# Layer norms of a transformer's second block: a shifted running sum on GpSimd, the last and first tile less the shift, one root, and another order of tiles

## The chip, the cores and the metric

The kernel runs on one core of a Trainium2 chip. The metric is the device time of one execution in microseconds, as the median of several runs. PE is the matrix engine (TensorE), DVE the vector engine (VectorE), ACT the scalar engine (ScalarE), POOL GpSimd, and SP the engine that issues the loads of weights.

## The reference, cut to what matters

Two blocks follow one another on 256 tokens of width 1024. The first (two mixers with RMS norms, two MLPs) is not touched. The second puts 16 meta tokens in front, which makes 272, and normalizes with means:

```python
def layer_norm(x, g, b):
    mu = jnp.mean(xf, -1, keepdims=True)
    var = jnp.mean(jnp.square(xf - mu), -1, keepdims=True)
    return (xf - mu) * lax.rsqrt(var + LN_EPS) * g + b

h = layer_norm(concat([meta, x]), emb_ln_g, emb_ln_b)         # mean_e
for i in range(2):
    u = h @ w_in[i]
    ...                                                       # attention and conv (with a norm of its own)
    h = layer_norm(ALPHA * h + mix, ln1_g[i], ln1_b[i])       # n10, n11
    f = swiglu(h, ...) if i == 0 else moe_swiglu(h, router, ...)
    h = layer_norm(ALPHA * h + f, ln2_g[i], ln2_b[i])         # n2, and the last norm
```

## The kernel before, in words

Activations lie with the 1024 features on partitions, as 8 tiles of 128 features by T = 272 tokens (RES holds the residual, XC centred tiles, SQ squares and normed tiles, RS the running sum). A sum over features is therefore a matmul with a matrix of ones, which leaves the sum over a tile's 128 features in every partition of a PSUM bank.

Weights stream through as 311 units of 1 MB, each 16 tiles of 128x128. ACT makes the high half `wh` of a unit (L1221) and DVE the low half `wl` (L1721, "the split"); three buffers hold them. A product is three matmuls (wh with the high half of x, wh with its low half, wl with the high half), 272 columns each. `gemm_lead` (L472 to L485) starts a gemm behind a norm: it takes tile 0 of the norm as soon as its high half is there (L472, L473), then its low half (L476), and then tile by tile the three products for four output tiles (L483 to L485). Further units go through L523 to L525.

There is no scheduler: each engine has a program of its own (`tensor_program`, `scalar_program`, `vector_program`, `gpsimd_program`, `sync_program`), in which the instructions stand in the order in which they run, with semaphore waits (`w.wait_ge(*m.of(...))`) between the engines. On DVE and ACT a split of the next unit is entered between the steps of a norm by the helper `sp` (`take`, `enter`, `hold`).

Four norms run through `shifted_norm`: mean_e behind the first block's last gemm, n10 and n11 behind the output gemms of the two layers (L2191 adds the bank into RES), n2 behind the dense feed-forward (L2216). They go in these steps:

- When tile 0 is in RES, a matmul sums it over the features, and ACT makes SH from it, the shift: the mean of tile 0 per token.
- For each tile DVE takes the shift off (L1940), ACT squares (L1402), and POOL adds: tiles into RS (L2548) and squares into SQ[0] (L2553).
- At the end PE's `last_sums` sums RS (L773) and the last tile (L778) into the mean's bank, and the squares (L780, L782) into the variance's. `keep_warm` (L431) issues products that nobody reads, to fill PE's waiting time: 1 and then 11.
- DVE makes d = mean - SH and d squared (L1955, L1957), v = variance + eps - d squared (L1960), and the first two centred tiles (L1950). ACT takes Ln and Exp (L1407, L1409) for a first value of the root, and DVE one Newton step (L1964 to L1968).
- DVE then makes each tile's normed value (L1973), centres a later tile (L1950), and makes the low half of the one before (L1985); ACT makes the high half (L1416). In n11 ACT writes RES instead (L1447), and the router follows on PE (L925 to L943).

`last_norm` at the end of the program (L1432 to L1440, L2001 to L2031) and the norms of the two conv layers (L1523, L1525) also take the root by Ln and Exp.

Of the kernel before, what the change touches and what calls it, by code (L numbers as in the profile page):

```python
# [11 lines left out]
ALU = mybir.AluOpType  # L12
# [3 lines left out]
P = 128  # L16
# [146 lines left out]
LOG_EXP = "natural_log_exp_and_others"  # L163
HUGE = 3.0e38
# [25 lines left out]
def model_kernel(nc, w_d, x_d, meta_d, small_d, const_d, look_d, out_d):  # L190
# [3 lines left out]
    with ctx:  # L194
# [206 lines left out]
        def tensor_program(w, pe):  # L401
# [354 lines left out]
            def shift_sum(stage, name):  # L756
                def pump(nt):
                    if nt == 2:
                        b, old = bank((name, "shift"), ("shift", name))
# [7 lines left out]
            def last_sums(stage, name):  # L767
                b, old = bank((name, "mean"), ("centred", (name, KD - 1)))
                if name == "n11":
                    held.add(b)  # L770
                vacant(old)
                w.wait_ge(*m.of("res_added", (name, KD - 2)))
# [432 lines left out]
        def scalar_program(w, act):  # L1205
# [187 lines left out]
            def shifted(name, nt):  # L1393

                if nt == 3:
                    w.wait_ge(*m.of("group", (name, "shift")))
                    act.activation(SH, bank((name, "shift"))[:, 0:T], ACT.Copy, scale=1.0 / P).then_inc(*m.inc("shift", name))
                if nt == KD - 1:
                    act.preload_act_table_set(LOG_EXP)
# [24 lines left out]
            def last_norm(tag, sem, keys):  # L1424
                act.preload_act_table_set(LOG_EXP)
# [9 lines left out]
                act.activation(SQ[:, 6, M:T], SQ[:, 5, M:T], ACT.Ln).then_inc(*m.inc("last_guess", "log"))  # L1435
                w.wait_ge(*m.of("last_guess", "log"))
                act.activation(BC[:, M:T], SQ[:, 6, M:T], ACT.Exp, scale=-0.5).then_inc(*m.inc("last_guess", "root"))
# [11 lines left out]
            def mix_layer(l):  # L1449
# [67 lines left out]
                act.preload_act_table_set(LOG_EXP)  # L1517
# [1223 lines left out]
```

## Time and profile before

| | us |
|---|---|
| median of 3 runs (1646.05 to 1647.68) | 1647.63 |
| the profiled execution's own time | 1647.6 |
| its span, from first to last instruction | 1645.8 |
| PE busy | 1614.5 (98%) |
| DVE busy | 1241.6 (75%) |
| ACT busy | 970.0 (59%) |
| POOL busy | 304.2 (18%) |
| mean granted clock of PE | 0.999 |

The time of an execution is 1.8 us longer than its span. Busy shares are means over the whole program; a norm is some ten microseconds, so it is read in the timeline of its own stretch. PE's busy time counts the products of `keep_warm`. In the timeline a line shows the start, the duration (for several instructions together their stretch), engine, line and operation, and in brackets the idle time ahead of it and what ended it; "x22" counts records, of which one fp32 matmul has two.

### The profile page before, as it was taken

Reading aid. Unit: us, or ns where it says so; the run is one execution under the profiler, and the core shown is the slowest. Engines: PE = TensorE matmul, PEld = TensorE weight load, DVE = VectorE, ACT = ScalarE, POOL = GpSimd, SP = SyncE. Lnnn points to the kernel's source line nnn. Section 1 sums busy time; section 2 is a strip of 40 time slices with the busy share of each in tenths; the row PEclk is TensorE's granted clock in tenths of the full one; section 3 lists DMA queues with packets and bytes.
Section 4 is the critical chain, followed back from the end, with each engine's and each line's share of the span. In section 5 each row is a group of like instructions: output and inputs, shape, how many; then the busy total and the mean of one; then the engine's idle time right before and its main releaser. Section 6 shows DMA issues by size and latency. Waiting matters only on the chain.

```text
span 1645.8 us, 27513 instructions
## 1 busy us (share of the span) xinstructions
PE 1614.5 (98%) x11020; PEld 1472.9 (89%) x11020; DVE 1241.6 (75%) x1766; ACT 970.0 (59%) x1377; POOL 304.2 (18%) x301
## 2 busy tenths in 40 slices
PE   7999999999999999999999999999999999999997
PEld 7988888898888889989999999999988888888886
DVE  6655776665667656998975545899988899998897
ACT  6556674346657633555554433555558677776775
POOL 1230652123226402052210002131110000000000
PEclk9999999999999999999999999999999999999999
DMA  7732455554245555433435444533439899988983
GB/s 282 255 126 80 179 197 188 197 206 162 103 159 195 185 179 211 164 132 126 154 132 201 171 175 169 180 143 136 173 118 342 332 341 343 340 334 332 351 340 125
DMA packets 50020, 339.73 MB, mean 206 GB/s; under 512 B 5403, under 2 KB 7611, under 8 KB 10208
## 3 DMA queue, kind: packets, MB, share of 16 engines
q1 hardware_dynamic: 47344, 328.79, 54.4%
q0 software_dynamic: 2544, 9.12, 1.7%
q8 instruction: 90, 1.47, 0.3%
q14 instruction: 42, 0.34, 0.1%
HBM read 336.76 MB, written 1.13 MB: 205 GB/s over the span
## 4 chain that ended last, share of the span: by engine, by line
PE 87%; DVE 4%; issue 4%; ACT 2%; POOL 2%; DMA 1%; SPq 0%; POOLq 0%; DVEq 0%; ACTq 0%
PE bank L549 12%; PE bank L523 8%; PE bank L525 8%; PE bank L524 8%; PE bank L547 7%; PE bank L979 5%; PE bank L980 5%; PE bank L981 5%; PE bank L1012 2%; PE bank L1011 2%; PE bank L1010 2%; PE bank L676 2%; PE bank L678 2%; PE bank L677 2%; PE bank L431 1%
## 5 line engine op out<-in xcount | busy, mean ns | idle before, releaser
L1721 DVE TENSOR_TENSOR wl<-stg,wh 128x2048 fp32r<-128x2048 f32 x310 | 712.7, 2302 | 208.1 <-ACT wh L1221 206.0
L1221 ACT ACTIVATE wh<-stg 128x2048 fp32r<-128x2048 f32 x310 | 592.8, 1913 | 178.9 <-PE bank L981 82.7
L523 PE MATMUL bank<-xx,wh 128*128 128x272 f32 (+1 forms) x778 | 225.3, 290 | 0.0
L525 PE MATMUL bank<-xx,wl 128*128 128x272 f32 (+1 forms) x778 | 223.1, 287 | 0.0
L524 PE MATMUL bank<-xx,wh 128*128 128x272 f32 (+1 forms) x778 | 223.0, 287 | 0.0
L549 PE MATMUL bank<-xx,wh 128*128 128x512 f32 x448 | 159.7, 396 | 0.0
L549 PE MATMUL bank<-H,wh 128*128 128x512 f32 x434 | 151.3, 390 | 0.0
L979 PE MATMUL bank<-wh,GH 128*128 128x512 f32 (+3 forms) x400 | 147.5, 369 | 0.0
L523 PEld LDWEIGHTS bank<-xx,wh 128*128 128x128 f32 x778 | 146.4, 188 | 1.1 <-issue 0.7
L524 PEld LDWEIGHTS bank<-xx,wh 128*128 128x128 f32 x778 | 147.4, 189 | 0.0
L525 PEld LDWEIGHTS bank<-xx,wl 128*128 128x128 f32 x778 | 146.4, 188 | 0.0
L980 PE MATMUL bank<-wh,GL 128*128 128x512 f32 (+3 forms) x400 | 146.3, 366 | 0.0
L981 PE MATMUL bank<-wl,GH 128*128 128x512 f32 (+3 forms) x400 | 146.2, 366 | 0.0
L676 PE MATMUL bank<-wh,xx 128*128 128x256 f32 x480 | 139.8, 291 | 1.0 <-DVE zm L1795 1.0
L678 PE MATMUL bank<-wl,xx 128*128 128x256 f32 x480 | 135.0, 281 | 0.0
L677 PE MATMUL bank<-wh,xx 128*128 128x256 f32 x480 | 134.7, 281 | 0.0
L547 PE MATMUL bank<-xx,wl 128*128 128x256 f32 x512 | 132.4, 279 | 0.0
L547 PE MATMUL bank<-H,wl 128*128 128x256 f32 x448 | 123.9, 282 | 0.0
L2523 POOL TENSOR_TENSOR fu<-ft 128x256 f32<-128x256 f32 x64 | 85.0, 1331 | 132.7 <-ACT ft L1369 132.7
L2081 DVE SCALAR_TENSOR_TENSOR CA<-HC,small,CA 128x272 f32<-128x272 f32 x240 | 107.6, 502 | 0.7
L547 PEld LDWEIGHTS bank<-xx,wl 128*128 128x128 f32 x512 | 96.5, 188 | 5.9 <-issue 0.3
L549 PEld LDWEIGHTS bank<-xx,wh 128*128 128x128 f32 x448 | 84.1, 188 | 17.2
(382 smaller groups left out, 3537.2 us busy)
## 6 DMA issues: line engine op xcount, KB each, us to landing
stg<-in_w SPq DMA_DIRECT2D x310, 1024.0 KB, 4.9
BT<-bias_scratch POOLq DMA_DIRECT2D x3, 1024.0 KB, 11.3
BT<-bias_scratch POOLq DMA_DIRECT2D x1, 2048.0 KB, 12.2
BB<-bias_scratch POOLq DMA_DIRECT2D x2, 1024.0 KB, 6.3
res<-in_x SPq DMA_DIRECT2D x1, 1024.0 KB, 7.2
stg<-in_w SPq DMA_DIRECT2D x2, 512.0 KB, 8.0
BB<-bias_scratch POOLq DMA_DIRECT2D x2, 512.0 KB, 7.1
out<-res SPq DMA_DIRECT2D x4, 256.0 KB, 3.3
```

Of the source, the lines that this page charges most:

```text
L523: pe.matmul(out, wh, xh(kt), start=kt == 0, stop=False)
L524: pe.matmul(out, wh, xl(kt), start=False, stop=False)
L525: ins = pe.matmul(out, wl, xh(kt), start=False, stop=kt == KT - 1)
L547: ins = pe.matmul(PS[b][:, 0:S], wl, high(kt), start=False, stop=False)
L549: ins = pe.matmul(out, wh, both(kt), start=False, stop=kt == KT - 1)
L676: pe.matmul(out, xh_t(kt, tt), wh, start=kt == 0, stop=False)
L678: ins = pe.matmul(out, xh_t(kt, tt), wl, start=False, stop=kt == KD - 1)
L979: pe.matmul(out, lh(kt, i), wh, start=kt == 0, stop=False)
L980: pe.matmul(out, ll(kt, i), wh, start=False, stop=False)
L981: ins = pe.matmul(out, lh(kt, i), wl, start=False, stop=kt == KD - 1)
L1221: act.activation(WH[u % NW][:, :], stg[u % NS][:, :], ACT.Copy).then_inc(*m.inc("w_high", u))
L1721: vec.tensor_tensor(WL[u % NW][:, :], stg[u % NS][:, :], WH[u % NW][:, :].bitcast(F32), ALU.subtract).then_inc(*m.inc("w_low_v", u))
```

## The change

In the four norms through `shifted_norm`:

- ACT makes two more copies of the shift: XC[3] = -7 SH, and XC[5] = 8 SH. POOL adds XC[3] into RS after tile 5, so that RS, with the tiles 0 to 6, holds their sum less seven shifts.
- After tile 6 DVE makes XC[6] = (ALPHA times) RES[7] - SH ahead of the last product (`less_shift`) and XC[2] = RES[0] - SH. When the last bank is there, `last_tile` adds it into XC[6]; the residual itself comes behind it. ACT squares XC[6] directly.
- PE sums RS and XC[6] into a bank "less", which is the sum over all features less the shift 1024 times. ACT squares its mean (into BC), and DVE needs only that for v; L1955 and L1957 are gone. A second bank, "mean", gets RS, XC[5] and XC[6]. `keep_warm` comes once, with 4.
- ACT takes one `Abs_reciprocal_sqrt` in place of Ln and Exp, here and in the conv norms and the last norm; the table set loaded in these places is another one.
- Tile 0 is centred from "less" (`first_tile`), ahead of the root; all others behind the root, each right before its normed value, in the order n0, c1, n1, low0, c2, n2, low1, and so on.

```diff
@@ last_sums (PE)
-                b, old = bank((name, "mean"), ("centred", (name, KD - 1)))
...
-                w.wait_ge(*m.of("res_added", (name, KD - 2)))
+                b, old = bank((name, "less"), ("centred", (name, 0)))
+                w.wait_ge(*m.of("res_added", (name, "shifted")))
                 pe.matmul(PS[b][:, 0:T], ones, RS, start=True, stop=False)
...
-                keep_warm(1)
-                w.wait_ge(*m.of("res", (stage, KD - 1)))
-                pe.matmul(PS[b][:, 0:T], ones, RES[:, KD - 1, 0:T], start=False, stop=True).then_inc(*m.inc("group", (name, "mean")))
                 w.wait_ge(*m.of("sq_added", (name, KD - 2)))
                 pe.matmul(PS[v][:, 0:T], ones, SQ[:, 0, 0:T], start=True, stop=False)
+                w.wait_ge(*m.of("last_tile", name))
+                pe.matmul(PS[b][:, 0:T], ones, XC[:, KD - 2, :], start=False, stop=True).then_inc(*m.inc("group", (name, "less")))
                 w.wait_ge(*m.of("shifted_sq", (name, KD - 1)))
                 pe.matmul(PS[v][:, 0:T], ones, SQ[:, KD - 1, 0:T], start=False, stop=True).then_inc(*m.inc("group", (name, "var")))
-                keep_warm(11)
+                f, old = bank((name, "mean"), ("centred", (name, KD - 1)))
...
+                w.wait_ge(*m.of("shift_8", name))
+                pe.matmul(PS[f][:, 0:T], ones, RS, start=True, stop=False)
+                pe.matmul(PS[f][:, 0:T], ones, XC[:, KD - 3, :], start=False, stop=False)
+                pe.matmul(PS[f][:, 0:T], ones, XC[:, KD - 2, :], start=False, stop=True).then_inc(*m.inc("group", (name, "mean")))
+                keep_warm(4)
@@ shifted, guess (ACT)
+                    act.activation(XC[:, 3, :], bank((name, "shift"))[:, 0:T], ACT.Copy, scale=(1.0 - KD) / P).then_inc(*m.inc("shift_7", name))
                 if nt == KD - 1:
-                    act.preload_act_table_set(LOG_EXP)
+                    act.preload_act_table_set(ROOT)
...
+                    act.activation(XC[:, KD - 3, :], SH, ACT.Copy, scale=float(KD)).then_inc(*m.inc("shift_8", name))
+                    w.wait_ge(*m.of("last_tile", name))
+                    act.activation(SQ[:, KD - 1, :], XC[:, KD - 2, :], ACT.Square, scale=D ** -0.5).then_inc(*m.inc("shifted_sq", (name, KD - 1)))
+                    return
...
             def guess(name):
+                w.wait_ge(*m.of("group", (name, "less")))
+                act.activation(BC[:, :], bank((name, "less"))[:, 0:T], ACT.Square, scale=1.0 / D).then_inc(*m.inc("mean_sq", name))
                 w.wait_ge(*m.of("var_out", name))
-                act.activation(SQ[:, 3, :], SQ[:, 2, :], ACT.Ln).then_inc(*m.step("table"))
-                w.wait_ge(*m.last("table"))
-                act.activation(BC[:, :], SQ[:, 3, :], ACT.Exp, scale=-0.5).then_inc(*m.inc("guess", name))
+                act.activation(BC[:, :], SQ[:, 2, :], ACT.Abs_reciprocal_sqrt).then_inc(*m.inc("guess", name))
@@ less_shift, last_tile, shifted_norm (DVE)
+                    ins = vec.scalar_tensor_tensor(XC[:, KD - 2, :], RES[:, KD - 1, :], scale, SH, ALU.mult, ALU.subtract)
+                ins.then_inc(*m.inc("less_shift", name))
+                vec.tensor_tensor(XC[:, 2, :], RES[:, 0, :], SH, ALU.subtract).then_inc(*m.inc("first_less", name))
...
+                vec.tensor_tensor(XC[:, KD - 2, lo:T], XC[:, KD - 2, lo:T], part, ALU.add).then_inc(*m.inc("last_tile", name))
...
-                vec.scalar_tensor_tensor(v, var, LN_EPS, d, ALU.add, ALU.subtract).then_inc(*m.inc("var_out", name))
-                centre(0)
-                centre(1)
+                vec.scalar_tensor_tensor(v, var, LN_EPS, BC[:, :], ALU.add, ALU.subtract).then_inc(*m.inc("var_out", name))
+                first_tile()
...
                     if kt == 0:
-                        centre(2)
-                    if 2 <= kt < KD - 1:
-                        centre(kt + 1)
+                        w.wait_ge(*m.of("group", (name, "mean")))
+                        centre(1)
                     if kt > 0:
                         low(kt - 1)
+                    if 0 < kt < KD - 1:
+                        centre(kt + 1)
@@ running (POOL)
                     pool.tensor_tensor(RS, RES[:, 0, :] if nt == 1 else RS, RES[:, nt, :], ALU.add).then_inc(*m.inc("res_added", (name, nt)))
+                    if nt == KD - 3:
+                        w.wait_ge(*m.last("res_added"))
+                        w.wait_ge(*m.of("shift_7", name))
+                        pool.tensor_tensor(RS, RS, XC[:, 3, :], ALU.add).then_inc(*m.inc("res_added", (name, "less")))
```

In the order of instructions the place is n10, between the output gemm's tile 6 and the first step behind the root. On DVE (xc is XC, dg the memory of SH, bank a PSUM bank), before:

```order
L2191 SCALAR_TENSOR_TENSOR res<-res,bank 128x272
L1940 TENSOR_TENSOR sq<-res,dg 128x272
L1721 TENSOR_TENSOR wl<-stg,wh 128x2048
L2191 SCALAR_TENSOR_TENSOR res<-res,bank 128x272
L1940 TENSOR_TENSOR sq<-res,dg 128x272
L1955 SCALAR_TENSOR_TENSOR sq<-bank,dg 128x272
L1957 TENSOR_TENSOR sq<-sq 128x272
L1960 SCALAR_TENSOR_TENSOR sq<-bank,sq 128x272
L1950 SCALAR_TENSOR_TENSOR xc<-bank,res 128x272 x2
L1964 TENSOR_TENSOR sq<-bc 128x272
```

and of the changed kernel, from the same tile 6 on:

```order
L2225 SCALAR_TENSOR_TENSOR res<-res,bank 128x272
L1958 TENSOR_TENSOR sq<-res,dg 128x272
L1967 SCALAR_TENSOR_TENSOR xc<-res,dg 128x272
L1969 TENSOR_TENSOR xc<-res,dg 128x272
L1733 TENSOR_TENSOR wl<-stg,wh 128x2048
L1974 TENSOR_TENSOR xc<-xc,bank 128x272
L2225 SCALAR_TENSOR_TENSOR res<-res,bank 128x272
L1992 SCALAR_TENSOR_TENSOR sq<-bank,bc 128x272
L1986 SCALAR_TENSOR_TENSOR xc<-bank,xc 128x272
L1995 TENSOR_TENSOR sq<-bc 128x272
```

Two steps that read the residual and the shift stand ahead of the split now, and behind the last tile only v and one centred tile stand ahead of the Newton step. On POOL in the same norm, before, from the addition of tile 4 on:

```order
L2548 TENSOR_TENSOR xc<-xc,res 128x272
L2553 TENSOR_TENSOR sq<-sq 128x272 x2
L2548 TENSOR_TENSOR xc<-xc,res 128x272
L2553 TENSOR_TENSOR sq<-sq 128x272
L2548 TENSOR_TENSOR xc<-xc,res 128x272
```

and of the changed kernel:

```order
L2590 TENSOR_TENSOR xc<-xc,res 128x272
L2601 TENSOR_TENSOR sq<-sq 128x272 x2
L2590 TENSOR_TENSOR xc<-xc,res 128x272
L2594 TENSOR_TENSOR xc<-xc 128x272
L2601 TENSOR_TENSOR sq<-sq 128x272
L2590 TENSOR_TENSOR xc<-xc,res 128x272
```

The addition L2594 stands between the sum of tile 5 and its square. On ACT one table load is added, in the router ahead of its Exp.

## Rows read from the trace of the kernel before

**Rows 1.** The page: parts 1 and 5 (columns: count; busy us, mean ns; idle before, releaser).

```profile
PE 1614.5 (98%) x11020; PEld 1472.9 (89%) x11020; DVE 1241.6 (75%) x1766; ACT 970.0 (59%) x1377; POOL 304.2 (18%) x301
...
L1721 DVE TENSOR_TENSOR wl<-stg,wh 128x2048 fp32r<-128x2048 f32 x310 | 712.7, 2302 | 208.1 <-ACT wh L1221 206.0
L1221 ACT ACTIVATE wh<-stg 128x2048 fp32r<-128x2048 f32 x310 | 592.8, 1913 | 178.9 <-PE bank L981 82.7
```

**Rows 2.** Timeline of mean_e: start us, us, engine, line, operation [idle before].

```profile
654.46 0.42 DVE L1921 TENSOR_TENSOR xc<-bank,bc 128x256 f32<-128x256 f32 x1 [1.30 <-PE bank L525]
...
656.90 4.91 PE L431 MATMUL bank<-consts 128*128 128x256 f32 x22
657.18 0.44 DVE L1960 SCALAR_TENSOR_TENSOR sq<-bank,sq 128x272 f32<-128x272 f32 x1
...
657.65 0.43 ACT L1407 ACTIVATE sq<-sq 128x272 f32<-128x272 f32 x1 [1.37 <-DVE sq L1960]
658.11 0.43 ACT L1409 ACTIVATE bc<-sq 128x272 f32<-128x272 f32 x1
...
660.00 0.50 DVE L1973 SCALAR_TENSOR_TENSOR sq<-xc,small,bc 128x272 f32<-128x272 f32 x1
...
663.15 0.29 PE L483 MATMUL bank<-xx,wh 128*128 128x272 f32 x1
```

**Rows 3.** Timeline of n2.

```profile
1034.92 0.62 PE L773 MATMUL bank<-xc,consts 128*128 128x272 f32 x2
...
1040.28 0.50 DVE L1973 SCALAR_TENSOR_TENSOR sq<-xc,small,bc 128x272 f32<-128x272 f32 x1
...
1043.44 0.29 PE L483 MATMUL bank<-xx,wh 128*128 128x272 f32 x1
```

**Rows 4.** Timeline of n10, on VectorE, GpSimd and TensorE.

```profile
824.21 0.51 DVE L1940 TENSOR_TENSOR sq<-res,dg 128x272 f32<-128x272 f32 x1
...
824.64 2.85 DVE L1721 TENSOR_TENSOR wl<-stg,wh 128x2048 fp32r<-128x2048 f32 x1
...
825.31 2.80 POOL L2548 TENSOR_TENSOR xc<-xc,res 128x272 f32<-128x272 f32 x1
...
828.26 0.70 PE L773 MATMUL bank<-xc,consts 128*128 128x272 f32 x2 [1.53 <-POOL xc L2548]
...
830.87 0.44 DVE L1960 SCALAR_TENSOR_TENSOR sq<-bank,sq 128x272 f32<-128x272 f32 x1
...
836.85 0.29 PE L483 MATMUL bank<-xx,wh 128*128 128x272 f32 x1
```

**Rows 5.** Timeline of n11 and the router's first products.

```profile
1198.26 0.76 POOL L2553 TENSOR_TENSOR sq<-sq 128x272 f32<-128x272 f32 x1
...
1201.05 0.44 DVE L1960 SCALAR_TENSOR_TENSOR sq<-bank,sq 128x272 f32<-128x272 f32 x1
...
1210.04 0.52 ACT L1447 ACTIVATE res<-sq,small 128x272 f32<-128x272 f32 x1 [0.37 <-DVE sq L1973]
...
1211.42 0.51 PE L925 MATMUL bank<-small,res 128*128 128x8 f32 x4
```

**Rows 6.** Timeline of ScalarE: a table load, its next instruction, and the router's Exp.

```profile
671.84 1.28 ACT L1487 ACT_TABLE_LOAD   x1
673.14 0.40 ACT L1487 ACTIVATE HC<-bank 128x272 f32<-128x272 f32 x1
...
1214.66 0.21 ACT L1573 ACTIVATE C<-C 128x2 f32<-128x2 f32 x1 [1.45 <-DVE C L2267]
```

**Rows 7.** Timeline of the last norm: VectorE's first step behind Exp.

```profile
1635.85 0.43 DVE L2015 TENSOR_TENSOR sq<-bc 128x256 f32<-128x256 f32 x1 [0.33 <-ACT bc L1437]
```

**Rows 8.** Granted clock (the number before the DMA share) by windows, and line L439.

```profile
826.00:828.00 2.00, 0.72 (x6) 0.50 (x4) 1.97 (x3) 0.48 (x1) 2.00 (x1) 1.00 0.56 238
1642.00:1643.00 1.00, 0.00 (x0) 0.00 (x0) 0.00 (x0) 0.00 (x0) 0.00 (x0) 0.68 0.72 242
...
L439 PE MATMUL bank<-res x10: 634/634/796, 8.4 to 12.4; 128*128 128x256 f32 x10
```

More of the change, by code:

```diff
@@ L758, in pump @@
                     if nt == 2:
-                        b, old = bank((name, "shift"), ("shift", name))
+                        b, old = bank((name, "shift"), ("shift_7", name))
                         vacant(old)
@@ L1434, in last_norm @@
                 w.wait_ge(*m.of("last_v"))
-                act.activation(SQ[:, 6, M:T], SQ[:, 5, M:T], ACT.Ln).then_inc(*m.inc("last_guess", "log"))
-                w.wait_ge(*m.of("last_guess", "log"))
-                act.activation(BC[:, M:T], SQ[:, 6, M:T], ACT.Exp, scale=-0.5).then_inc(*m.inc("last_guess", "root"))
+                act.activation(BC[:, M:T], SQ[:, 5, M:T], ACT.Abs_reciprocal_sqrt).then_inc(*m.inc("last_guess", "root"))
                 for kt in range(6):
@@ L1522, in silu @@
                     w.wait_ge(*m.of("var_out", name))
-                    act.activation(SQ[:, 5, :], SQ[:, 4, :], ACT.Ln).then_inc(*m.step("table"))
-                    w.wait_ge(*m.last("table"))
-                    act.activation(BC[:, :], SQ[:, 5, :], ACT.Exp, scale=-0.5).then_inc(*m.inc("guess", name))
+                    act.activation(BC[:, :], SQ[:, 4, :], ACT.Abs_reciprocal_sqrt).then_inc(*m.inc("guess", name))
                     sp.one_ahead()
@@ L1929, in evac_y @@
                         shifted("mean_e", nt)
+                        if nt == KD - 2:
+                            less_shift("mean_e", None)
                 walk(KD, 32, evac_y)
@@ L1937, in shifted @@
                     w.wait_ge(*m.of("shift", name))
+                if nt == KD - 1:
+                    return
                 for kt in SHIFTED.get(nt, ()):
@@ L1942, in shifted, with less_shift @@
                     sp.hold()
+            def less_shift(name, scale):
+                if scale is None:
+                    ins = vec.tensor_tensor(XC[:, KD - 2, :], RES[:, KD - 1, :], SH, ALU.subtract)
+                else:
+                    ins = vec.scalar_tensor_tensor(XC[:, KD - 2, :], RES[:, KD - 1, :], scale, SH, ALU.mult, ALU.subtract)
+                ins.then_inc(*m.inc("less_shift", name))
+                vec.tensor_tensor(XC[:, 2, :], RES[:, 0, :], SH, ALU.subtract).then_inc(*m.inc("first_less", name))
@@ L1944, in shifted_norm, with last_tile @@
+            def last_tile(name, part, lo):
+                w.wait_ge(*m.of("less_shift", name))
+                vec.tensor_tensor(XC[:, KD - 2, lo:T], XC[:, KD - 2, lo:T], part, ALU.add).then_inc(*m.inc("last_tile", name))
             def shifted_norm(name, gname, l, low):
-                d, v, t = SQ[:, 1, :], SQ[:, 2, :], SQ[:, 3, :]
-                mean, var = bank((name, "mean"))[:, 0:T], bank((name, "var"))[:, 0:T]
+                v, t = SQ[:, 2, :], SQ[:, 3, :]
+                less, mean, var = (bank((name, part))[:, 0:T] for part in ("less", "mean", "var"))
@@ L1949, in centre, with first_tile @@
                 def centre(kt):
                     vec.scalar_tensor_tensor(XC[:, kt, :], mean, -1.0 / D, RES[:, kt, 0:T], ALU.mult, ALU.add).then_inc(*m.inc("centred", (name, kt)))
+                def first_tile():
+                    w.wait_ge(*m.of("first_less", name))
+                    vec.scalar_tensor_tensor(XC[:, 2, :], less, -1.0 / D, XC[:, 2, :], ALU.mult, ALU.add).then_inc(*m.inc("centred", (name, 0)))
                 w.wait_ge(*m.last("res"))
-                w.wait_ge(*m.of("group", (name, "mean")))
@@ L1954, in shifted_norm @@
                 w.wait_ge(*m.of("sq_added", (name, KD - 2)))
-                vec.scalar_tensor_tensor(d, mean, 1.0 / D, SH, ALU.mult, ALU.subtract).then_inc(*m.step("v_step"))
-                w.wait_ge(*m.last("v_step"))
-                vec.tensor_tensor(d, d, d, ALU.mult).then_inc(*m.step("v_step"))
-                w.wait_ge(*m.last("v_step"))
+                w.wait_ge(*m.of("mean_sq", name))
                 w.wait_ge(*m.of("group", (name, "var")))
-                vec.scalar_tensor_tensor(v, var, LN_EPS, d, ALU.add, ALU.subtract).then_inc(*m.inc("var_out", name))
@@ L2193, in evac_o @@
                     shifted(f"n1{l}", nt)
+                    if nt == KD - 2:
+                        w.wait_ge(*m.of("y_out", (before, KD - 1)))
+                        less_shift(f"n1{l}", ALPHA)
                 walk_late(KD, KD, evac_o)
@@ L2215, in evac_d @@
                     w.wait_ge(*m.of("y_out", ("n10", nt)))
+                    if nt == KD - 1:
+                        last_tile("n2", bank(("dn", nt))[:, 0:T], 0)
                     vec.scalar_tensor_tensor(RES[:, nt, :], RES[:, nt, :], ALPHA, bank(("dn", nt))[:, 0:T], ALU.mult,
@@ L2218, in evac_d @@
                     shifted("n2", nt)
+                    if nt == KD - 2:
+                        w.wait_ge(*m.of("y_out", ("n10", KD - 1)))
+                        less_shift("n2", ALPHA)
                 walk(KD, 22, evac_d)
```

22 lines of the change are left out of this document (17 added, 5 removed).

## The prediction

> **What bounds the kernel now.** I read the page first, then the stretch around each of the four norms in the timeline, then the chain of waits there. TensorE is busy for 98% of the span, and ScalarE's largest wait, before the high halves of the weights, is for a buffer that TensorE still reads (82.7 us of 178.9): matmuls, not DMA, set the pace [rows 1]. So a norm costs what lies between the last product in front of it and the first steady product behind it, and a microsecond saved there carries through to the end. Busy time hides this, because L431 fills the gaps with products that nobody reads.
>
> In mean_e, VectorE was idle for 1.30 us when the last tile's bank came (654.46), v (L1960) starts at 657.18, Ln and Exp follow 0.46 apart, the first normed tile (L1973) starts at 660.00, and the second tile's first full product (L483) at 663.15 [rows 2]. The 22 records of L431 end at 661.81, so the lead could not begin much earlier; yet the second tile, which needs a low half from VectorE, is what starts the steady run. From n0 to it pass 3.15 us here, and 3.16 us in n2 (1040.28 to 1043.44) [rows 2, 3].
>
> n10 is different. VectorE's shift of tile 6 (0.51) is followed at once by a weight split of 2.85 us, against a mean of 2.30 [rows 1, 4]. GpSimd's addition for RS next to it takes 2.80, against 0.76 alone [rows 4, 5]. So the two engines exclude each other while both work from SBUF. TensorE idles 1.53 us for that RS and starts the sums at 828.26. In this norm GpSimd is on the path.
>
> **The change, part by part.** A step of 128x272 takes 0.44 to 0.51 on VectorE and 0.43 on ScalarE, one behind the other every 0.46; GpSimd's addition holds the shared way for about 0.67 of its 0.76 (both [rows 2, 4, 5]; 0.67 is my estimate). A pair of fp32 matmuls takes about 0.46: 22 records of 256 columns take 4.91 [rows 2], a little more at 272.
>
> *One root for Ln and Exp.* The step from L1407 to L1409 is 0.46 [rows 2]. The root's own price is not in the trace. Its nearest rows are Ln, at 0.43 [rows 2], and an activation with a small operand, at 0.52 [rows 5]; below 0.43 it can hardly lie, since the tile is the same. I take 0.43: 0.46 less per norm, at worst 0.37.
>
> *The path to v in mean_e and n2.* Before: scale, residual, L1940, Square, and L1955, L1957, L1960. Now the last tile comes less the shift by one VectorE step (0.46 ahead of the residual), ScalarE squares it, TensorE makes the "less" pair and the last square's pair, ScalarE squares the mean, and v follows. In mean_e: scale 654.46, last tile to 655.36, less pair to about 655.9, the mean's square to 656.45 beside the other pair (which ends near 656.4), v near 656.7 against 657.18: 0.5 less. In n2 the four pairs run in a row from 1034.92 [rows 3], to about 1036.8, and v comes about 0.4 earlier. The two new steps behind tile 6 (less_shift, first_less: 0.9 together) fit into VectorE's idle time there, 1.30 [rows 2]; without that cover they would cost up to 0.9.
>
> *The order of tiles.* Each centre now stands right before its norm, so every norm waits for its centre, and the low half of tile 1 comes ahead of tile 3's centre. I count n0, c1, n1, low0, c2, n2, low1 at the starts of [rows 2] and the same steps' spacing: n0 to low1 2.33, plus its 0.49 and 0.13 for the semaphore, so 2.95 to the second tile, against 3.15. So mean_e gains 0.5 + 0.46 + 0.2 = **1.15**, and n2 0.4 + 0.46 + 0.2, rounded down to **1.0**. The extra products behind the sums are 4 instead of 12, with two pairs more in the mean's group; they end by about 660.0, ahead of the lead at about 660.2, so they hold nothing.
>
> *n10.* Two VectorE steps with two SBUF inputs now stand ahead of the split, and one GpSimd addition ahead of the squares of tile 5. If the engines take turns (as the rows of the split and of RS show), the queue from 824.35 is: shift 6 0.42, new addition 0.67, less_shift 0.49, square 5 0.67, first_less 0.42, RS 0.67, which ends at 827.5 (0.6 earlier than now [rows 4]); then the split to 829.8; then the square of tile 6 to 830.45. The last tile comes only behind the split, at 829.75. The pairs of SQ0, less and the last square start near 830.6, and v at about 832.2, against 830.87 [rows 4]: 1.3 later. Root 0.46 less, so n0 at 834.55. The second tile was at 836.85 in this view because L431 and the lead held TensorE rather than VectorE; now it is n0 + 2.95 = 837.5. By the chain's modelled start of the same product, 0.15 later than the row, that is **+0.55**.
>
> *n11.* The same queue without a split. Square 6 ends at about 1200.3 (now 1198.26 + 0.76), v at about 1202.05 against 1201.05; root 0.46 less; n0 +0.55. Tiles 1 and 2 no longer have their centres ready, which costs 0.6 more by tile 7. The last output starts at 1210.04 + 1.17 = 1211.2 and ends 0.52 later; the router's last tile on TensorE starts at 1211.42 now [rows 5], then at about 1211.8: **+0.37**.
>
> *Route.* The root's table lacks Exp, and one more table load (1.28 [rows 6]) stands before the router's Exp at 1214.66, which waits 1.45 us for VectorE [rows 6]. A load started at about 1213.6 ends at 1214.9, near the shifted start of Exp: **0**. Behind a load of the trace that someone waits for, the next instruction starts 0.02 later (671.84 + 1.28, then 673.14 [rows 6]). The Trainium skill (ScalarE: Activation LUTs, What ACT_TABLE_LOAD costs) gives about 1.28 for the load and 1.38 more for a drain; by it the router's Exp would come up to 1.3 later, and the sum would be 0 to 1.3 higher. The trace agrees on the 1.28 and shows no drain behind it, so I keep 0.
>
> *Tail.* VectorE's step L2015 waits 0.33 for Exp [rows 7]: about **-0.3**. The conv norms stand beside a split and gain 0. ScalarE's copies of -7 and 8 shifts are early; RS waits for the first only from tile 5 on.
>
> **Sum.** -1.15 - 1.0 + 0.55 + 0.37 - 0.3 = -1.5. The profiled execution took 1647.6, and the median of the runs shown is 1647.63, so 1646.1.
>
> **Rivals.** (A) is the sum: 0.50.
>
> (B) The new additions are hidden in n10 and n11: the split starts when it does now, or GpSimd gets through early, and TensorE's wait of 1.53 [rows 4] shrinks with RS. Then n10 gives -0.8 and n11 -0.3: -1.15 - 1.0 - 0.8 - 0.3 - 0.3 = -3.55, so 1644.0. For it: RS is ready earlier in my own count, and the idle 1.53. Against it: the split now stands behind two more steps by the program's order. 0.20. What the Trainium skill (SBUF — State Buffer, SBUF: two separate sides) says, that the one which starts first keeps the shared port for its whole instruction, is a rule for A; the 2.80 for 0.76 agrees.
>
> (C) The other side: TensorE's clock falls in n10. Between the RS pair and the last pairs there would now be an idle stretch of about 2.4 us, and fewer products fill the time behind it. The granted clock fell to 0.68 at 1642 to 1643, after TensorE had stopped at the end, and the first products of the run, L439, were granted half: ten of them start 4.0 us apart, 0.44 each, against 0.22 for L431 [rows 2, 8]. At half speed three pairs cost 1.4 more, and the lead's first 4.6 us give 2.3: +3.7, so 1649.8; in n11 too, 1653.5. The point from which it decides: a granted clock under 1.00 behind the wait. Against it: it stayed 1.00 through the 1.53 [rows 8]. 0.08. The Trainium skill (TensorE: Matmul & The Clock Gate, Part 1: The HAM clock gate) has two levels, 1.2 and 2.4 GHz, and an idle engine loses the upper; no run here shows that for such a gap.
>
> (D) mean_e and n2 gain little, because TensorE is held in the lead by products that fill or by the weights' low half, which VectorE splits later: about +0.6 in all, 1648.2. For it: L431 ends late today. 0.14.
>
> (E) The change does not do what it says: the root takes 1 us or a load falls on the path of each norm (+1.28 x 4, less the gains): up to 1651. 0.08; the order of instructions shows only one more load, off the norms.
>
> **How the numbers follow.** A measurement here tells about 0.2%, 3.3 us, from no change. Faster (under 1644.3) takes most of B and a little of A: 0.19. Slower (over 1650.9) takes half of C and of E: 0.09. The rest is the same: 0.72. The range from 1643.8 to 1648.9 takes in A, B and D with the bounds of the root and of the turns (up to 0.9 more per norm).
>
> **What would show it.** Right: v near 656.7 and the second tile near 662.0; in n10, the split's start near 827.5 and the second tile 0.5 later than now. Wrong: a split in n10 that still starts near 824.6, a granted clock under 1.00, a root over 0.6, or an L431 that ends as the lead's releaser in mean_e.

## The result: 1649.3 us, against 1647.18 of the kernel before

Over 20 executions each, the changed kernel took 1649.3 us (median; 1647.55 to 1651.0) and the kernel before 1647.18 (1646.05 to 1648.17). The ratio is 1.0013, with a 95% interval of 1.0007 to 1.0019: 1.2 to 3.1 us slower. The prediction was 1646.1, its range ended at 1648.9, and slower by over 0.2% had a chance of 0.09. What came is 0.13% slower: 0.4 us above the range, and within the 0.2% that the forecast had counted as no change, at 0.72.

The two profiled executions differ by less: spans of 1646.4 and 1645.8. To see where, one needs a clock that both traces share. ScalarE has instructions that start as soon as TensorE releases them; the same ones in both traces show how far TensorE has come. Of the kernel before (the timeline, ScalarE; ahead of mean_e, late in mixer 0, ahead of n10, in the feed-forward, behind n2, late in mixer 1, in the experts, in the last norm):

```profile
648.92 1.92 ACT L1221 ACTIVATE wh<-stg 128x2048 fp32r<-128x2048 f32 x1 [1.11 <-PE bank L525]
...
728.39 0.40 ACT L1497 ACTIVATE SG<-bank 128x272 f32<-128x272 f32 x1 [1.25 <-PE bank L525]
...
820.77 1.92 ACT L1221 ACTIVATE wh<-stg 128x2048 fp32r<-128x2048 f32 x1 [0.24 <-PE bank L525]
...
886.77 0.40 ACT L1559 ACTIVATE dt<-bank 128x272 f32<-128x272 f32 x1 [0.30 <-PE bank L525]
...
1060.27 1.92 ACT L1221 ACTIVATE wh<-stg 128x2048 fp32r<-128x2048 f32 x1 [2.28 <-PE bank L525]
...
1127.12 0.38 ACT L1497 ACTIVATE SG<-bank 128x256 f32<-128x256 f32 x1 [2.07 <-PE bank L525]
...
1223.67 1.92 ACT L1221 ACTIVATE wh<-stg 128x2048 fp32r<-128x2048 f32 x1 [2.20 <-PE bank L981]
...
1633.20 0.38 ACT L1432 ACTIVATE bc<-bank 128x256 f32<-128x256 f32 x1 [1.77 <-PE bank L1123]
```

and the same instructions of the changed kernel:

```profile
648.28 1.92 ACT L1228 ACTIVATE wh<-stg 128x2048 fp32r<-128x2048 f32 x1 [1.12 <-PE bank L526]
...
727.05 0.40 ACT L1511 ACTIVATE SG<-bank 128x272 f32<-128x272 f32 x1 [0.17 <-PE bank L526]
...
820.18 1.92 ACT L1228 ACTIVATE wh<-stg 128x2048 fp32r<-128x2048 f32 x1 [0.24 <-PE bank L526]
...
887.12 0.40 ACT L1571 ACTIVATE dt<-bank 128x272 f32<-128x272 f32 x1 [0.30 <-PE bank L526]
...
1059.95 1.92 ACT L1228 ACTIVATE wh<-stg 128x2048 fp32r<-128x2048 f32 x1 [1.20 <-PE bank L526]
...
1127.70 0.38 ACT L1511 ACTIVATE SG<-bank 128x256 f32<-128x256 f32 x1 [2.06 <-PE bank L526]
...
1224.69 1.92 ACT L1228 ACTIVATE wh<-stg 128x2048 fp32r<-128x2048 f32 x1 [2.20 <-PE bank L988]
...
1634.18 0.38 ACT L1448 ACTIVATE bc<-bank 128x256 f32<-128x256 f32 x1 [1.77 <-PE bank L1130]
```

Take the differences: -0.64, -1.34, -0.59, +0.35, -0.32, +0.58, +1.02, +0.98, and +0.6 at the end of the span. The first has nothing to do with the change: it is there from the start of the program, and the changed kernel's own traces differ there by up to 1.4 us. What a stretch costs is the step from one number to the next:

| stretch | forecast | measured |
|---|---|---|
| mean_e, up to mixer 0 | -1.15 | -0.70 |
| rest of mixer 0 | 0 | +0.75 |
| n10 and what follows it | +0.55 | +0.94 |
| n2, up to mixer 1 | -1.0 | -0.67 |
| rest of mixer 1 | 0 | +0.90 |
| n11, router, first experts | +0.37 | +0.44 |
| experts and tail | -0.3 | -0.42 |
| sum | -1.5 | +1.24 |

So the two norms that were to gain do gain, by two thirds of the forecast, and both give it back, and a little more, some sixty microseconds later. n10 loses more than forecast.

**mean_e.** The changed kernel's timeline, to be read beside [rows 2] (whose times are 0.64 later for the start alone):

```profile
656.12 0.44 DVE L1992 SCALAR_TENSOR_TENSOR sq<-bank,bc 128x272 f32<-128x272 f32 x1 [1.08 <-PE bank L781]
...
656.60 0.43 ACT L1425 ACTIVATE bc<-sq 128x272 f32<-128x272 f32 x1 [0.68 <-DVE sq L1992]
...
657.16 1.89 PE L432 MATMUL bank<-consts 128*128 128x256 f32 x8
...
658.49 0.50 DVE L2004 SCALAR_TENSOR_TENSOR sq<-xc,small,bc 128x272 f32<-128x272 f32 x1
658.91 0.43 DVE L1982 SCALAR_TENSOR_TENSOR xc<-bank,res 128x272 f32<-128x272 f32 x1
...
659.38 0.50 DVE L2004 SCALAR_TENSOR_TENSOR sq<-xc,small,bc 128x272 f32<-128x272 f32 x1
...
660.68 0.50 DVE L2004 SCALAR_TENSOR_TENSOR sq<-xc,small,bc 128x272 f32<-128x272 f32 x1
...
661.10 0.49 DVE L2017 SCALAR_TENSOR_TENSOR xx<-sq,small,xx 128x272 fp32r<-128x272 f32 x1
...
661.74 0.36 PE L484 MATMUL bank<-xx,wh 128*128 128x272 f32 x1 [0.30 <-ACT xx L1432]
...
668.77 2.28 DVE L1733 TENSOR_TENSOR wl<-stg,wh 128x2048 fp32r<-128x2048 f32 x1
```

v came at 656.12, 0.42 earlier than before with the start taken off (0.5 forecast). The root took 0.43, as chosen, and n0 follows v by 2.37. L432 now ends at 659.05 and holds nobody. But the low half of tile 1 (661.10) starts 2.61 behind n0, not 2.33, and TensorE's second tile 3.25 behind, not 2.95: 0.1 more than before, where 0.2 less had been counted. Each normed tile (L2004) waits for the centre (L1982) right ahead of it and starts 0.47 behind it. One tile takes VectorE 1.30 us, from 659.38 to 660.68. Of the kernel before, VectorE:

```profile
661.60 0.50 DVE L1973 SCALAR_TENSOR_TENSOR sq<-xc,small,bc 128x272 f32<-128x272 f32 x1
...
662.77 0.50 DVE L1973 SCALAR_TENSOR_TENSOR sq<-xc,small,bc 128x272 f32<-128x272 f32 x1
...
669.05 2.28 DVE L1721 TENSOR_TENSOR wl<-stg,wh 128x2048 fp32r<-128x2048 f32 x1
```

There a tile took 1.17. One centre more stands in the loop, too. Together that adds up: from n0 to the split of the next unit pass 10.28 us, against 9.05. The split starts at 668.77, and in the kernel before at 669.05, which is 668.41 without the start. **VectorE ends the norm 0.36 us later, while TensorE begins its run 0.77 earlier.**

**Mixer 0.** There this decides. The timeline of ScalarE, TensorE and VectorE:

```profile
672.87 0.40 ACT L1501 ACTIVATE HC<-bank 128x272 f32<-128x272 f32 x1
...
731.69 0.51 PE L827 MATMUL bank<-K,Q 64*128 64x145 f32 x2
...
732.12 0.40 DVE L2103 TENSOR_TENSOR ML<-bank,MH 128x256 fp32r<-128x256 f32 x1
...
732.57 0.51 PE L827 MATMUL bank<-K,Q 64*128 64x145 f32 x2 [0.37 <-DVE ML L2103]
...
733.02 0.71 PE L837 MATMUL bank<-consts,Lb 128*16 128x128 f32 x5
```

and of the kernel before, VectorE and TensorE:

```profile
725.18 0.50 DVE L2056 CUSTOM_DVE_ANT_0 Lb<-bank,BB,ns 128x273 f32<-128x273 f32 x1 [0.92 <-PE bank L830]
...
733.03 0.62 PE L820 MATMUL bank<-K,Q 64*128 64x145 f32 x4
733.59 0.71 PE L830 MATMUL bank<-consts,Lb 128*16 128x128 f32 x5
```

The delay goes by way of ScalarE. Behind the high half of VectorE's last normed tile ScalarE has eight writes of the residual, a table load, and then L1501, the first step of the mixer, which starts at 672.87; before, it started at 673.14 [rows 6], or 672.50 without the start, 0.37 earlier. VectorE goes on at 673.37, behind 2.31 us without work. (The profile puts this wait down to a TensorE bank; the lead's last product had ended at 672.52, ScalarE's step ends at 673.27.) From there to L2103 VectorE has convolution taps and splits, and waits only twice, for ScalarE, 0.26 and 0.40 us near 726. In the kernel before it waited there for TensorE, 0.92 us at 725.18; that reserve is used up. So L2103, a VectorE step of the attention, comes at 732.76 on the clock of the trace before, where the same step started at 732.69, and TensorE, which is 0.7 ahead, waits for it. In the kernel before the same products show no wait. From the first of them to L837 (before, L830) pass 1.33 us, against 0.56: what TensorE had gained is gone here (from -1.34 to -0.59).

In mixer 1 TensorE waits for a ScalarE step of the attention, and did not before:

```profile
1099.37 0.80 PE L811 MATMUL bank<-PTb,V 16*64 16x128 f32 x8 [0.53 <-ACT PTb L1477]
```

**n10**, the place of the order of instructions ahead of the prediction, to be read beside [rows 4]:

```profile
824.07 1.01 DVE L1967 SCALAR_TENSOR_TENSOR xc<-res,dg 128x272 f32<-128x272 f32 x1
...
825.00 1.01 DVE L1969 TENSOR_TENSOR xc<-res,dg 128x272 f32<-128x272 f32 x1
...
825.66 0.96 POOL L2590 TENSOR_TENSOR xc<-xc,res 128x272 f32<-128x272 f32 x1
...
825.93 2.85 DVE L1733 TENSOR_TENSOR wl<-stg,wh 128x2048 fp32r<-128x2048 f32 x1
826.59 2.80 POOL L2601 TENSOR_TENSOR sq<-sq 128x272 f32<-128x272 f32 x1
...
826.77 0.70 PE L773 MATMUL bank<-xc,consts 128*128 128x272 f32 x2 [0.64 <-POOL xc L2590]
...
829.54 0.70 PE L777 MATMUL bank<-sq,consts 128*128 128x272 f32 x2 [2.07 <-DVE res L2225]
...
831.33 0.44 DVE L1992 SCALAR_TENSOR_TENSOR sq<-bank,bc 128x272 f32<-128x272 f32 x1 [1.85 <-PE bank L781]
...
836.94 0.36 PE L484 MATMUL bank<-xx,wh 128*128 128x272 f32 x1 [0.31 <-ACT xx L1432]
```

The engines take turns as forecast: less_shift and first_less (L1967, L1969) take 1.01 each beside GpSimd's additions, GpSimd gets RS (L2590, 0.96) through ahead of the split, and the last squares wait out the split (2.80). The split starts at 825.93, or 826.5 on the clock of the trace before (827.5 forecast), v at 831.9 (832.2), the second tile at 837.5 (837.5). That last match is luck in part: n0 came 0.3 earlier than forecast (834.3 against 834.55), and from it to the second tile passed 3.25 us, not 2.95. Between the sum RS and the last sums TensorE idles 2.07 us (2.4 forecast). Behind the second tile 0.3 more is lost. VectorE's next split starts 1.83 later than before there, the start taken off; that this is what the feed-forward lost was not tried by itself.

In n11 and the tail the forecast held: +0.44 and -0.4. The extra table load in the router starts at 1214.25 in this trace and no TensorE wait follows it.

### The profile page after: what moved, and what is told of

Same layout as the page of the kernel before. It is cut to its first block, busy times and chain, and to the rows that moved or that the text cites. A ratio compares the mean times of both kernels' runs of the same rounds, so it can differ in the third digit from the quotient of the medians.

```text
span 1646.4 us, 27451 instructions
## 1 busy us (share of the span) xinstructions
PE 1609.3 (98%) x10980; PEld 1465.0 (89%) x10980; DVE 1246.5 (76%) x1766; ACT 972.2 (59%) x1383; POOL 308.3 (19%) x305
## 3 DMA queue, kind: packets, MB, share of 16 engines
HBM read 336.76 MB, written 1.13 MB: 205 GB/s over the span
## 4 chain that ended last, share of the span: by engine, by line
PE 79%; DVE 10%; issue 4%; ACT 3%; POOL 1%; DMA 1%; SPq 0%; DVEq 0%; POOLq 0%; ACTq 0%
PE bank L550 12%; PE bank L548 7%; PE bank L524 7%; PE bank L526 7%; PE bank L525 7%; PE bank L986 5%; PE bank L987 5%; PE bank L988 5%; DVE wl L1733 3%; DVE CA L2113 3%; PE bank L1019 2%; PE bank L1018 2%; PE bank L1017 2%; PE bank L677 2%; PE bank L679 2%
```

## The experiments

All kernels ran beside the kernel before. Medians are given less that kernel's beside them, and the cost by stretch is read as above. The columns are the first 728 us without the start, the rest of mixer 0, n10, n2, the rest of mixer 1, n11, and what follows:

| run | mean_e | mixer 0 | n10 | n2 | mixer 1 | n11 | tail | sum | median |
|---|---|---|---|---|---|---|---|---|---|
| changed kernel | -0.70 | +0.75 | +0.94 | -0.67 | +0.90 | +0.44 | -0.42 | +1.24 | +2.12 |
| e1_again | -0.70 | +0.76 | +0.93 | -0.66 | +0.87 | +0.53 | -0.43 | +1.30 | +1.76 |
| e2_order | -0.61 | 0 | +2.00 | -0.59 | 0 | +0.49 | -0.50 | +0.79 | +0.52 |
| e3_pool | -0.58 | +0.76 | +0.13 | -0.21 | +0.89 | +0.05 | -0.40 | +0.64 | +0.60 |
| e4_warm | -0.70 | +0.73 | +0.94 | -0.67 | +0.90 | +0.60 | -0.36 | +1.44 | +2.08 |
| e5_order_warm | -0.61 | -0.01 | +0.84 | -0.58 | 0 | +0.48 | -0.53 | -0.41 | -0.22 |
| e6_root_only | 0 | -0.01 | +0.02 | 0 | 0 | +0.18 | -0.47 | -0.28 | +0.03 |
| e7_first | -0.70 | +0.76 | +2.14 | -0.66 | +0.90 | +0.45 | -0.40 | +2.49 | +2.56 |
| e8_best | -0.48 | 0 | -0.08 | -0.10 | 0 | -0.31 | -0.39 | -1.36 | -1.13 |
| e9_root_fill | -0.44 | -0.02 | -0.42 | -0.45 | +0.01 | -0.79 | -0.52 | -2.63 | -2.74 |

A sum leaves out the start, which by these traces scatters from -1.24 to +0.41 against the trace before.

**e1_again.** No edit.

> The changed kernel once more, as the base for the three runs beside it. Its 20 executions had a median of 1649.3 us (1647.55 to 1651.0), and those above 1650 had a mean granted clock of 0.997 or 0.998, those near 1648.2 one of 0.999, where the profiled one (1648.15) shows no fall before the end. Theory of the clock: again a spread of about 3 us, the longer executions at the lower mean clock, and a trace of one of them shows the granted clock under 1.00 behind a norm. Rival: the spread lies in the start or in the loads of weights, and a trace of a longer execution shows the clock at 1.00 throughout the norms.

1649.06 us (1647.85 to 1650.3; before 1647.30), ratio 1.0010 [1.0001, 1.0019]. Three of its 11 executions had a mean clock of 0.997. The one traced kept 1.00 in the norms, so the rival was left open here.

**e2_order.** The centre is made one tile ahead again.

```diff
                     if kt == 0:
                         w.wait_ge(*m.of("group", (name, "mean")))
                         centre(1)
+                        w.wait_ge(*m.of("normed_y", (name, 0)))
+                        centre(2)
+                    if 2 <= kt < KD - 1:
+                        centre(kt + 1)
                     if kt > 0:
                         low(kt - 1)
-                    if 0 < kt < KD - 1:
-                        centre(kt + 1)
```

> The changed kernel with one difference: the centred tile is made one tile ahead again (n0, c1, c2, n1, low0, n2, c3, low1, ...). Theory that VectorE's end of the norm sets the mixers behind mean_e and n2 (its step per tile is 1.30 us instead of 1.17, and TensorE waits for VectorE's L2103 some 60 us later): VectorE ends the norm 0.8 us earlier in each, that wait goes, and the time falls by 1.2 to 1.7 us against the changed kernel run beside it, 0.3 of it in n11. Rival, that TensorE's second tile alone sets the end: the second tile comes about 0.1 later with this order, and the time is the same within 0.3.

1647.82 us, ratio 1.0008 [0.9999, 1.0017], 1.24 less than e1_again. The second tile came 0.1 later in both norms, and the losses in both mixers, 0.75 and 0.90, were gone. In mean_e the split starts at 667.73, with a start of -0.79: 0.53 earlier than before instead of 0.36 later. So the order of the tiles is shown as the cause of both losses. ScalarE's first step of the mixer is 0.53 earlier too, so the run does not part the two engines: that the delay goes by way of ScalarE is read from the trace alone. What was not expected stood in n10. By windows (the granted clock is the number before the DMA share), first e2_order:

```profile
828.00:829.00 1.00, 0.27 (x1) 0.30 (x2) 0.67 (x2) 0.43 (x1) 0.59 (x1) 1.00 0.00 0
829.00:830.00 1.00, 1.00 (x4) 0.72 (x4) 0.00 (x0) 0.00 (x0) 0.00 (x0) 0.51 0.87 164
...
832.00:833.00 1.00, 1.00 (x4) 0.79 (x4) 0.85 (x3) 0.86 (x2) 0.00 (x0) 0.79 0.09 33
```

then its products there:

```profile
829.50 1.11 PE L779 MATMUL bank<-xc,consts 128*128 128x272 f32 x2
830.41 1.11 PE L781 MATMUL bank<-sq,consts 128*128 128x272 f32 x2
```

Behind 2.07 us without a product TensorE ran at 0.50, which is 1.2 of 2.4 GHz, for some 3 us, and a pair of products came every 0.91 instead of 0.46. n10 cost 2.00 where the changed kernel's trace has 0.94. Seven of the 11 executions had a mean clock of 0.997 or less, two of them (1652.9) one of 0.994.

**e3_pool.** TensorE sums the seven shifts; GpSimd's addition goes.

```diff
                 pe.matmul(PS[b][:, 0:T], ones, RS, start=True, stop=False)
+                w.wait_ge(*m.of("shift_7", name))
+                pe.matmul(PS[b][:, 0:T], ones, XC[:, 3, :], start=False, stop=False)
...
-                pe.matmul(PS[f][:, 0:T], ones, XC[:, KD - 3, :], start=False, stop=False)
+                pe.matmul(PS[f][:, 0:T], ones, SH, start=False, stop=False)
...
-                        pool.tensor_tensor(RS, RS, XC[:, 3, :], ALU.add).then_inc(*m.inc("res_added", (name, "less")))
```

(ScalarE's copy of eight shifts goes as well, since SH itself now stands in the mean.)

> The changed kernel without GpSimd's addition of seven shifts: TensorE sums XC[3] as one more pair instead, and SH takes the place of XC[5] in the mean. Theory that GpSimd and VectorE take turns in n10 and n11: one turn of 0.93 us goes, the squares of tile 6 end before the split in n10, and v comes 0.7 to 1.0 us earlier there and 0.5 to 0.9 earlier in n11; 0.2 is lost in mean_e and n2 for the extra pair: the time falls by 0.8 to 1.5 us against the changed kernel run beside it. Rival, that the split and the two new VectorE steps set n10: less than 0.4.

1647.90 us, ratio 1.0002 [0.9993, 1.0011], 1.16 less than e1_again. n10 fell from 0.93 to 0.13 and n11 from 0.53 to 0.05: the one GpSimd instruction was most of the loss in n10 and nearly all of it in n11. n2 gave back 0.45 for the extra pair.

**e4_warm.** Products that nobody reads in TensorE's idle stretches.

```diff
+                keep_warm({"n10": 1, "n11": 3}.get(name, 0))
                 w.wait_ge(*m.of("res_added", (name, "shifted")))
                 pe.matmul(PS[b][:, 0:T], ones, RS, start=True, stop=False)
+                keep_warm(4 if name == "n10" else 0)
...
-                keep_warm(4)
+                keep_warm(5)
```

> The changed kernel with products that nobody reads put back into TensorE's idle stretches: 1 ahead of the sum RS and 4 behind it in n10, 3 ahead of it in n11, and 5 instead of 4 at the end of each. Theory of the clock (TensorE idles 2.07 us in n10 and 0.65 us ahead of each lead, and in some executions the granted clock falls there): the mean granted clock is 0.999 in nearly all executions, the spread falls to about 2 us, and the median falls by 1.0 to 1.6 us. Rival (the spread has nothing to do with the idle stretches): median and spread as in the changed kernel run beside it, within 0.4.

1649.38 us (1646.87 to 1649.61). No execution had a mean clock under 0.998, as the theory wanted, but the median did not fall: it is 0.3 above e1_again's. Nor did the spread (2.7 us against 2.5). The mean is 0.4 lower (1648.75 against 1649.12). In 11 executions the scatter of the start, over 1.5 us, covers much of what a fall in a part of them is worth. By median and spread the expectation failed.

**e5_order_warm.** Both edits.

> The changed kernel with the tile order one ahead (as in the run before) and with products put back into TensorE's idle stretches of n10 and n11. With the order alone the traced execution had the granted clock at 0.50 for about 3 us in n10, behind an idle stretch of 2.07 us; 7 of its 11 executions had a mean clock of 0.997 or less, and two took 1652.9. Theory of the clock: with that idle time filled no execution is under 0.998 and none is above 1649.5; the trace shows 1.00 in n10; n10 costs 0.9 us against the kernel before, as in the changed kernel without a fall, and no longer 2.0. Rival, that the fall comes from elsewhere: again several at 0.997 or less.

1646.70 us (1645.89 to 1647.63; before 1646.92), ratio 0.9997 [0.9988, 1.0006]. The clock stayed at 1.00 in n10, which cost 0.84; no execution was under 0.998 or above 1647.63. With e2_order this parts the clock from the order of tiles: the fall in n10 was worth about 1.2 us in the trace.

**e6_root_only.** The kernel before with the root alone.

```diff
-                act.activation(SQ[:, 3, :], SQ[:, 2, :], ACT.Ln).then_inc(*m.step("table"))
-                w.wait_ge(*m.last("table"))
-                act.activation(BC[:, :], SQ[:, 3, :], ACT.Exp, scale=-0.5).then_inc(*m.inc("guess", name))
+                act.activation(BC[:, :], SQ[:, 2, :], ACT.Abs_reciprocal_sqrt).then_inc(*m.inc("guess", name))
```

(and likewise in the conv and last norms, with the table set loaded there)

> The kernel before with Ln and Exp replaced by the one root, in all norms, and nothing else of the change. By the changed kernel's trace the root saves about 0.46 us on ScalarE's path, so v to the first normed tile takes 2.37 us instead of 2.83. Theory that VectorE's end of the norm sets the mixers: VectorE too ends 0.46 earlier, so each of the four norms gains 0.4 to 0.5, the tail 0.3 to 0.4, and the time falls by 1.5 to 2.2 us against the kernel before. Rival, that TensorE's 22 records of products that nobody reads hold the lead: the four norms gain 0.2 or less each, about 1.0 in all.

1646.95 us, ratio 0.9998 [0.9989, 1.0007]. VectorE had n0 0.35 us earlier in mean_e, less the start, and yet three norms gained nothing. The products that nobody reads were still there, by the timeline of TensorE:

```profile
655.98 4.91 PE L432 MATMUL bank<-consts 128*128 128x256 f32 x22
```

They end at 660.89, again 0.92 before [rows 2], just as the start was: what they hold does not move when VectorE does. The rival held, and more strictly than it was put.

**e7_first.** XC[2] behind the last tile.

```diff
-                vec.tensor_tensor(XC[:, 2, :], RES[:, 0, :], SH, ALU.subtract).then_inc(*m.inc("first_less", name))
...
+                vec.tensor_tensor(XC[:, 2, :], RES[:, 0, :], SH, ALU.subtract).then_inc(*m.inc("first_less", name))
                 w.wait_ge(*m.last("res"))
                 w.wait_ge(*m.of("sq_added", (name, KD - 2)))
```

> The changed kernel with one VectorE step moved: XC[2] = RES[0] - SH comes behind the last tile's residual, where VectorE waits 1.85 us for the variance, and no longer ahead of the split. Theory that VectorE and GpSimd take turns: the split of n10 starts one turn (0.93 us) earlier, so v comes 0.7 to 1.0 earlier there; in n11 the sum RS and the last square come 0.4 to 0.9 earlier; mean_e and n2 lose 0.1 or less. The time falls by 1.0 to 1.7 us against the changed kernel (1649.06 and 1649.3). Rival, that GpSimd's queue alone sets n10: less than 0.4.

1649.48 us, ratio 1.0010 [1.0001, 1.0019]: no gain. The split did start a turn earlier, but it then stood ahead of GpSimd's RS, by the timelines of VectorE and GpSimd:

```profile
825.15 2.85 DVE L1733 TENSOR_TENSOR wl<-stg,wh 128x2048 fp32r<-128x2048 f32 x1
...
825.82 2.81 POOL L2590 TENSOR_TENSOR xc<-xc,res 128x272 f32<-128x272 f32 x1
...
828.77 0.87 PE L773 MATMUL bank<-xc,consts 128*128 128x272 f32 x2 [2.48 <-DVE res L2225]
```

RS waits out the split, TensorE idles 2.48 us instead of 0.64 and 2.07, and its clock fell there too (0.50 from about 829 to 832); n10 cost 2.14. How much the step would give without the fall was not tried by itself. VectorE's two short steps ahead of the split had let GpSimd through.

**e8_best.** The edits of e2, e3 and e7 together, with `keep_warm(5)` at the end of the sums.

> All three together: order one ahead, TensorE sums the seven shifts, XC[2] behind the last tile, and 5 products instead of 4 behind the sums. If the theories hold each norm gains against the kernel before: mean_e and n2 about 0.6 each, n10 0.3 to 0.9, n11 0 to 0.5, tail 0.35: 1.9 to 2.9 us less than the kernel before, so 1644.4 to 1645.4, as long as the granted clock holds in n10. If it falls there in some executions, those are 1 us or more longer, and the median is about 1646.

1645.79 us (1645.09 to 1646.35), ratio 0.9991 [0.9982, 1.0000], 0.4 above the range expected. Every stretch is at or below the kernel before, but mean_e, n2 and n10 gave less than hoped: 0.48, 0.10 and 0.08. The extra pair costs its 0.46 in n2.

**e9_root_fill.** The kernel of e6 with fewer products that nobody reads.

```diff
-                keep_warm(11)
+                keep_warm(9)
```

> The kernel before with the root in place of Ln and Exp (which gave nothing in the four norms), and with 9 instead of 11 products that nobody reads at the end of each norm's sums (0.87 us less). Theory that these products held the lead, so that the root's 0.46 us could not come through: now mean_e, n2 and n10 gain 0.35 to 0.5 each, n11 0.1 to 0.3, and with the tail's 0.4 the time falls by 1.4 to 2.0 us against the kernel before. Rival, that something else holds the lead or the mixers (weights, VectorE's splits): the four norms gain 0.2 or less in all, and the time is 0.3 to 0.6 less than before.

1644.58 us (1643.79 to 1645.41; before 1647.32), ratio 0.9984 [0.9975, 0.9993]. mean_e, n10 and n2 gained 0.44, 0.42 and 0.45, n11 0.79, more than expected. The products now end at 660.48, by the timeline of TensorE:

```profile
656.43 4.05 PE L432 MATMUL bank<-consts 128*128 128x256 f32 x18
```

This is faster than both kernels, with none of the change but its root. How much the fewer products would give by themselves, without the root, was not tried.

**e10_again, e11_again, e12_again.** The changed kernel three times more, for traces.

> The changed kernel for one more trace. In two traces of it the granted clock stayed at 1.00 up to the end, and the four norms with what follows them cost 1.62 and 1.70 us against the kernel before; its median is 1.8 to 2.1 us above. Theory that the clock falls in n10 in a part of its executions (by 1.1 us each, as in the traces with the other order and with the moved step): at least one of the three traces of this call shows 0.50 in n10, and n10 costs about 2.0 there instead of 0.93. Rival, that it never falls in this kernel: 0.93 and a clock of 1.00 in all three.

> The changed kernel for one more trace, with the same expectations as the one before it in this call: the granted clock in n10 at 0.50 and a cost of about 2.0 us there in at least one of the three, or 1.00 and 0.93 in all.

> The changed kernel for one more trace, with the same expectations as the two before it in this call: the granted clock in n10 at 0.50 and a cost of about 2.0 us there in at least one of the three, or 1.00 and 0.93 in all.

They took 1647.61, 1648.46 and 1649.39. The first two cost 0.94 and 0.92 in n10 and kept 1.00 there. The third had a mean clock of 0.997. By windows:

```profile
830.00:831.00 1.00, 1.00 (x4) 0.77 (x3) 0.00 (x0) 0.00 (x0) 0.00 (x0) 0.50 0.54 205
...
833.00:834.00 1.00, 1.00 (x6) 0.84 (x5) 0.82 (x3) 1.00 (x2) 0.00 (x0) 1.00 0.00 0
```

and its products behind the idle stretch, which is 2.07 us again:

```profile
829.37 1.12 PE L777 MATMUL bank<-sq,consts 128*128 128x272 f32 x2 [2.07 <-DVE res L2225]
```

n10 cost 2.19: 1.26 more than in the four other traces of this kernel. So the clock does fall in the changed kernel, in a part of its executions.

## Why the prediction was wrong

**The step that failed** is in its first paragraph: that a norm ends with the first steady product, so that "a microsecond saved there carries through to the end". TensorE is not the only engine that leaves a norm. Its second tile came 0.7 us earlier in mean_e and n2, but VectorE's last low half came 0.36 later in mean_e, and with it ScalarE's first step of the mixer. The mixer needs all of them, and VectorE reached its step of the attention there no earlier than before (732.76 against 732.69, the start taken off). e6_root_only moved VectorE alone and gained nothing, the changed kernel moved TensorE alone and kept nothing, e2_order moved both and kept 0.6 in each norm, and e9_root_fill moved both by about 0.4 and kept it.

**The order of tiles** was priced from its effect on tile 1 alone, and with the wrong sign there. It counted the steps and not the wait of each norm for the centre just ahead of it: 0.13 us for each tile. e2_order, which takes that wait away, shows that without it nothing is lost in the mixers. The forecast had a cost of this order by tile 7, 0.6 us, in n11, and none in the three other norms. No row gives the 0.13 that it adds for the semaphore; the changed kernel's trace has 0.15 there (661.59 to 661.74).

**n10** was forecast at +0.55 and cost 0.92 to 0.94 in four traces. The turns were right (split, RS, v and second tile each within about a microsecond; the second tile to 0.1, by two errors that cancelled). Two of its sums are a little off: the queue's terms add up to 827.69, not 827.5, and the last step to +0.50, not +0.55. The missing part lies behind the second tile, where the forecast had stopped looking, as in the first error. e3_pool confirms the share of the GpSimd addition.

**Rival C**, the clock, happened, at a chance put at 0.08. It was priced at 3.7 us for n10; the trace has 1.26, because the clock was back at 1.00 before the lead began, and only the pairs ran at half. The forecast took the first products of the run for products at half clock; their spacing is doubled, but the trace lists 1.00 over them. The change needs no fall to make the kernel slower: +1.24 to +1.45 without one. A mean clock of 0.997 or less stood in 9 of 34 executions of the changed kernel, and in none of the 81 executions of the kernel before that list it. That count is too low, since the traced executions of e2_order and e7_first have the fall and list 0.998. The listed clocks of the 34 have a mean of 0.9981, those of the 81 of 0.9987, and the fall of e12_again takes 0.0010 (1.7 of 1648 us): by these numbers some 0.6 falls per execution, an estimate. At 1.26 us each that is some 0.7 more, so about 2.0 by the traces; the medians say 2.12 and 1.76, each uncertain by a microsecond or more. That "against it: it stayed 1.00 through the 1.53" was no bound for 2.07.

**Rival D** (mean_e and n2 gain little, 1648.2) came nearest; its cause, the weights' low half, was close, but it was a step of the attention that TensorE waited for. **Right** were v in both early norms, the root at 0.43, n11 (+0.37 forecast, 0.44 to 0.53 measured), the tail, and that the router's table load costs nothing. The range was too narrow because every one of its cases let the gain of mean_e and n2 through or left it out; none let it turn into a loss elsewhere.

## What to carry to other kernels

Before you add up what a shorter stage gains, find every engine that carries work out of it, and ask for each when it is free and whether the next stage waits for it: a gain on one engine is worth the least of them. An order that puts a producer right ahead of its consumer costs a wait on every item, even on one engine, and a short GpSimd instruction between VectorE steps from the same memory costs a turn. Where filler products keep an engine busy, shorten them together with what they cover, and look whether new gaps arise that they no longer fill.

## What the runs showed of the hardware

The granted clock fell behind an idle stretch of 2.07 us (and a 0.6 us one shortly before it) in one of five traces of the changed kernel and in the one of e2_order, and behind 2.48 us in e7_first; in four traces the same 2.07 us left it at 1.00. So one trace without a fall does not exclude one. Once it had fallen, it was at 0.50 for some 3 us, with TensorE busy again from the first of them. The Trainium skill (TensorE: Matmul & The Clock Gate, Part 1: The HAM clock gate) has the throttled clock as the default, which activity releases; the three traces with a fall agree, with 0.50 behind the idle stretch. The start of the program, which no kernel here changes, scatters by 1.65 us between traces, more than most of the effects studied, and has to be taken off before two traces are compared.
